# Expert weights loaded into dying attention buffers, a loop head at another slot, and two GpSimd steps at another time, in a two-layer decoder trunk

## What is computed

```python
def moe_swiglu(hn, w_router, w_gate, w_up, w_down):
    logits = (xt @ w_router).astype(jnp.float32)
    top_logit, top_idx = lax.top_k(logits, TOP_K)        # 2 of 8 experts
    gates = jax.nn.softmax(top_logit, axis=-1)
    ...
    def expert_block(args):
        xb, e = args
        hid = jax.nn.silu(xb @ w_gate[e]) * (xb @ w_up[e])
        return hid @ w_down[e]
    ...
    y = jnp.zeros((T, D), hn.dtype).at[row_tok].add(yb * row_g[:, None])
```

## Time and profile before

| | us |
|---|---|
| median of 3 runs | 1325.47 (1324.51 to 1325.51) |
| the profiled execution | 1328.43 |
| its span, first to last instruction | 1326.6 |
| PE busy | 1290.7 (97%) |
| DVE busy | 677.4 (51%) |
| ACT busy | 252.0 (19%) |
| POOL busy | 63.7 (5%) |
| mean granted TensorE clock | 0.996 |
| DMA over the span | 442.93 MB, 334 GB/s |

### The profile page before, as it was taken

The page is one execution under the profiler, slowest core; times in us unless marked ns, Lnnn a source line. Parts: engine busy times, 40 slices in busy tenths (PEclk is TensorE's granted clock), DMA queues, the critical chain, the costliest instruction groups (busy, mean ns, idle before and its releaser), DMA issues.

```text
span 1326.6 us, 38823 instructions
## 1 busy us (share of the span) xinstructions
PE 1290.7 (97%) x17222; PEld 1007.6 (76%) x17222; DVE 677.4 (51%) x943; ACT 252.0 (19%) x386; POOL 63.7 (5%) x50
## 2 busy tenths in 40 slices
PE   9999999999999999999999999999999999999898
PEld 9998899988767567567766955866875695696597
DVE  5875655554875556165145335516614614542661
ACT  5564544443643100000000000000000000000000
POOL 1001000000000330000000000000000000002600
PEclk9999999999999899999999999999999999999999
DMA  9867565565522999999999999999999999999992
GB/s 320 261 213 227 187 191 181 180 223 179 186 93 72 388 419 418 416 419 417 416 418 417 416 416 410 417 417 409 417 416 405 417 416 402 417 417 416 405 398 103
DMA packets 114224, 442.93 MB, mean 334 GB/s; under 512 B 9284, under 2 KB 55700, under 8 KB 83348
## 3 DMA queue, kind: packets, MB, share of 16 engines
q1 hardware_dynamic: 107904, 424.75, 81.3%
q10 hardware_dynamic: 4820, 11.53, 2.5%
q0 software_dynamic: 1344, 4.20, 0.8%
HBM read 434.12 MB, written 12.08 MB: 336 GB/s over the span
## 4 chain that ended last, share of the span: by engine, by line
PE 90%; DVE 4%; ACT 3%; issue 3%; DMA 0%; ACTq 0%; DVEq 0%
PE bank L2003 22%; PE bank L2051 22%; PE bank L2021 20%; PE bank L1553 7%; PE bank L1555 7%; PE bank L1554 7%; ACT w_hi L661 1%; DVE w_lo L955 1%; PE bank L1800 1%; PE bank L1711 1%; DMA const<-in_shape_constants 0%; PE bank L1976 0%; ACT ht_hi L689 0%; DVE sums L1478 0%; PE bank L1855 0%
## 5 line engine op out<-in xcount | busy, mean ns | idle before, releaser
L2003 PE MATMUL bank<-raw,xT 128*32 128x384 f32 (+1 forms) x2688 | 260.5, 532 | 10.7 <-issue 9.8
L2003 PEld LDWEIGHTS bank<-raw,xT 128*32 128x32 f32 x2688 | 110.8, 110 | 154.3 <-issue 133.8
L2021 PE MATMUL bank<-more_ring,xT 128*32 128x256 f32 (+1 forms) x3072 | 207.0, 354 | 0.4 <-issue 0.4
L955 DVE TENSOR_TENSOR w_lo<-raw,w_hi 128x2048 fp32r<-128x2048 f32 x62 | 141.4, 2289 | 98.0 <-ACT w_hi L661 98.0
L1473 DVE TENSOR_TENSOR sums<-more_ring 128x768 f32<-128x768 f32 (+1 forms) x64 | 69.8, 1090 | 234.3 <-PE bank L2021 193.3
L2051 PE MATMUL bank<-more_ring,hidT 128*32 128x256 f32 x3072 | 170.7, 379 | 0.0
L2021 PEld LDWEIGHTS bank<-more_ring,xT 128*32 128x32 f32 x3072 | 147.4, 110 | 25.2 <-issue 5.0
L2051 PEld LDWEIGHTS bank<-more_ring,hidT 128*32 128x32 f32 x3072 | 150.4, 110 | 18.1
L1553 PE MATMUL bank<-ht_hi,w_hi 128*128 128x256 f32 x464 | 128.7, 277 | 1.5 <-DVE ht_lo L969 1.5
L2051 PE MATMUL bank<-raw,hidT 128*32 128x256 f32 x2304 | 129.2, 379 | 0.0
L1555 PE MATMUL bank<-ht_hi,w_lo 128*128 128x256 f32 x464 | 128.3, 277 | 0.0
(11 more groups left out here) (312 smaller groups left out, 1603.1 us busy)
## 6 DMA issues: line engine op xcount, KB each, us to landing
more_ring<-in_moe_w_up SPq DMA_DIRECT2D x64, 1024.0 KB, 17.4
more_ring<-in_moe_w_down SPq DMA_DIRECT2D x64, 1024.0 KB, 16.2
raw<-in_moe_w_gate SPq DMA_DIRECT2D x64, 768.0 KB, 18.3
more_ring<-in_moe_w_up SPq DMA_DIRECT2D x64, 768.0 KB, 18.2
raw<-in_moe_w_gate SPq DMA_DIRECT2D x48, 1024.0 KB
raw<-in_moe_w_down SPq DMA_DIRECT2D x48, 1024.0 KB, 18.9
more_ring<-in_moe_w_gate SPq DMA_DIRECT2D x16, 1024.0 KB
raw<-in_hgrn_w_in SPq DMA_DIRECT2D x15, 1024.0 KB, 11.8
```

Source lines behind the costliest of these rows:

```text
L955: nc.vector.tensor_tensor(w_lo[:, slot, :], raw[:, slot_raw, :], plain(w_hi[:, slot, :]), SUB).then_inc(split_ready, 1)
L2003: ins = nc.tensor.matmul(out_banks[j][GTOK * c:GTOK * c + GTOK, 0:w], xT[:, j, kt, :], chunk[:, c], start=kt == 0, stop=kt == KT - 1)
L2021: ins = nc.tensor.matmul(dst[GTOK * c:GTOK * c + GTOK, :], rows, columns[:, c], start=opens, stop=pair == PAIRS - 1, skip_group_check=True)
```

## The change

Five edits, in SBUF layout and in waits; no computation is added or removed.

- `w_hi` and `w_lo` move up behind the first 16240 floats (`LOW`) of the region; the stage memory of the attention now starts at the bottom, right under `more_ring`, in the order `bias_rev`, `kT`, `aqT`, `vt`, and so on.
- SP issues the loads that follow the eight of `raw` when all logits are computed (12 signals of `logits_full`), and, from the first load on that reaches past `bias_rev`, `kT` and `aqT` (`KEYS_END`, load 12 in the code), when the attention products are done (`turned`). The waits for `chunk_used` and `h_part` go.
- The PE loop's head goes from slot 128 to slot 0.
- GpSimd waits, after its gathers, for all hidden-layer transposes of the last item before it multiplies and adds.
- Routing scratch (`hnT` and the small tensors) lies in the region of `w_lo`; `e_silu`, `e_hid` and `hidT` no longer share space with it as before, the small tensor `over` is renamed `over_cap`, and the scratch of a Square (L680) is a buffer of its own.

```diff
-LOOP_SLOT = 128
+LOOP_SLOT = 0
+
+LOW = 16240
...
-        dense = ExitStack()
-        w_hi = sb(dense, "w_hi", [P, SPLIT, CW], f32r)
-        w_lo = sb(dense, "w_lo", [P, SPLIT, CW], f32r)
+        with ExitStack() as over:
+
+            sb(over, "low", [P, LOW])
+            w_hi = sb(over, "w_hi", [P, SPLIT, CW], f32r)
+            w_lo = sb(over, "w_lo", [P, SPLIT, CW], f32r)
...
         bias_rev = sb(s, "bias_rev", [P, QH, 2 * P])
-        vt = sb(s, "vt", [P, TT, 256])
-
         kT = sb(s, "kT", [P, KVH, T])
         aqT = sb(s, "aqT", [P, QH // 2, T])
-
+        vt = sb(s, "vt", [P, TT, 256])
...
+        with ExitStack() as over:
+
+            sb(over, "below_lo", [P, LOW + SPLIT * CW])
+            hnT = sb(over, "hnT", [P, KT, T])
+            rank0 = sb(over, "rank0", [P, TT, E])
...
+        with ExitStack() as over:
+
+            squares = sb(over, "squares", [P, D])
+        early_second = sb(ctx, "early_second", [P, TT, D])
...
+        KEYS_END = QH * 2 * P + KVH * T + QH // 2 * T
...
-            sp.wait_ge(chunk_used, C_MOE)
-            sp.wait_ge(h_part, 3 * 4)
             for k in range(in_raw, N_UP):
+                if k == in_raw:
+                    sp.wait_ge(logits_full, 3 * KVH)
+                if k < first_lap and LOAD_ENDS[k - 1] <= RAW * CW + KEYS_END < LOAD_ENDS[k]:
+                    sp.wait_ge(turned, TURN_ATT)
                 if k >= first_lap:
                     wait_used(0, k)
                 load(0, k)
...
+            pool.wait_ge(hidT_ready, n_before * (2 * GRPS) + 2 * GRPS)
+            pool.sem_inc(pool_pace, 1)
             for i in range(2):
                 for t in range(TT):
                     pool.wait_ge(fetched[t][i], 16)
...
-                    spare = hidT[1][:, 0:2, :, :].rearrange("p g m t -> p (g m t)") if i == 3 else xs[:, t, :]
+                    spare = squares[:, :] if i == 3 else xs[:, t, :]
```

More of the change, by code:

```diff
@@ L254, in build_program @@
         s.close()
-        dense.close()
-        more_ring = sb(ctx, "more_ring", [P, RING - RAW * CW])
+        with ExitStack() as over:
+            sb(over, "below_lo", [P, LOW + SPLIT * CW])
+            hnT = sb(over, "hnT", [P, KT, T])
+            rank0 = sb(over, "rank0", [P, TT, E])
+            top = sb(over, "top", [P, TT, 8])
+            topi = sb(over, "topi", [P, TT, 8], u32)
+            topf = sb(over, "topf", [P, TT, 2])
+            hot = sb(over, "hot", [P, TT, 2, E])
+            mask = sb(over, "mask", [P, TT, E])
+            rank = sb(over, "rank", [P, TT, E])
+            big = sb(over, "big", [P, TT, E])
+            more = sb(over, "more", [P, 2, E])
+            which = sb(over, "which", [P, E + 1])
+            nth = sb(over, "nth", [1, 2, E])
+            whose = sb(over, "whose", [1, 2, E])
+            it = sb(over, "it", [1, 8, 2, E])
+            itf = sb(over, "itf", [1, 32])
+        more_ring = sb(ctx, "more_ring", [P, RING - RAW * CW])
+        ones = sb(ctx, "ones", [P, E + 1])
+        base = sb(ctx, "base", [P, E])
+        late = sb(ctx, "late", [P, E])
+        over_cap = sb(ctx, "over_cap", [P, E + 1])
+        steps = sb(ctx, "steps", [P, 44])
+        quarters = sb(ctx, "quarters", [P, 4])
+        with ExitStack() as over:
+            squares = sb(over, "squares", [P, D])
+        early_second = sb(ctx, "early_second", [P, TT, D])
         xT = sb(ctx, "xT", [P, GRPS, KT, GTOK])
@@ L260, in build_program @@
         slot = sb(ctx, "slot", [P, TT, 2, 4], u32)
-        steps = sb(ctx, "steps", [P, 44])
-        quarters = sb(ctx, "quarters", [P, 4])
         passed = sb(ctx, "passed", [P, TT, 2, 44])
@@ L269, in build_program @@
         end_selT = sb(ctx, "end_selT", [CAP, T])
[L270 to L294, removed]
+        e_silu = sb(ctx, "e_silu", [P, GRPS, 512])
+        e_hid = sb(ctx, "e_hid", [P, GRPS, 512])
+        hidT = [sb(ctx, f"hidT{i}", [P, GRPS, n // GTOK, GTOK]) for i, (at, n) in enumerate(SUPERS)]
         banks = [ctx.enter_context(nc.psum_tensor(f"bank{i}", [P, 512], f32)) for i in range(8)]
@@ L1339, in _ @@
             nc.vector.memset(ones[:, :], 1.0)
-            nc.vector.memset(over[:, :], 0.0)
+            nc.vector.memset(over_cap[:, :], 0.0)
             nc.vector.tensor_scalar(base[:, :], iota8, float(CAP), None, MUL)
@@ L1381, in _ @@
             then(ins)
-            then(nc.vector.tensor_tensor(over[:, 1:E + 1], more[:, 0, :], more[:, 1, :], ADD))
-            then(nc.vector.tensor_tensor_scan(which[:, :], ones[:, :], over[:, :], 0.0, MUL, ADD))
+            then(nc.vector.tensor_tensor(over_cap[:, 1:E + 1], more[:, 0, :], more[:, 1, :], ADD))
+            then(nc.vector.tensor_tensor_scan(which[:, :], ones[:, :], over_cap[:, :], 0.0, MUL, ADD))
             nc.vector.tensor_scalar(itf[0:1, 16:17], which[0:1, E:E + 1], float(E), None, ADD)
```

## The result

The changed kernel takes 1337.3 us (median of 5 runs, 1331.29 to 1339.31) beside 1325.47 us for the kernel before; the ratio over all runs is 1.0075, 95% interval 1.0059 to 1.0091. The profiled execution took 1331.29 us with a span of 1329.5, against 1328.43 and 1326.6 before: some 3 us more in the profiles, 10 in the ratio. The profile of after is thus the quickest of its runs, and I read it for places rather than for the total.

What follows compares the result with a forecast made beforehand. It took the expert loop as bound by TensorE, DMA queues nearly as full. Adds 3.0, slot 0.8 and loads 0.3 us off the median 1325.47 gave 1321.4, stated as 1321.0 (1319.3 to 1322.7 at 0.60; 8 in 10: 1317.3 to 1324.3).

Steps and rivals of the forecast that it cites:

- The new places of buffers: SBUF layout: moved buffers, routing scratch among them, keep every shape and instruction; costed at nothing.
- the list of what the new profile would show: Signs for each step: late adds, ordinary last item, DMA without pause from 415 us, small gap gone, items of 108.2 us.
- Slot 0: PE expert loop's head: the fetch boundary 62 records behind it goes away; 0 to 1.5 us gain, taken as 0.8.
- rival (3): Expert loop's two fast phases: an added boundary in each arrives late, 0.5 us each, 8 us in all, 1329.0; chance 0.08.
- three signs that I had named for a failure: Items over 109 us, a microseconds-long gap inside the last item's matmul run, or VectorE's last addition waiting for GpSimd.
- The adds: Last item's first fast phase: moving GpSimd's adds later frees VectorE's sums; 3.0 us in the median, up to 6.6 profiled.
- gap of 2.77 us in the profiled execution of before: Last item's first fast phase: PE issue gap taken as late code; with clock loss about 3.6 us, profiled execution only.
- my 22 us: VectorE beside GpSimd's eight instructions: full-length exclusion would cost some 22 us, sum near 1303; ruled out, given no chance.
- The early loads: SP's ten loads after the raw half: start 13 to 16 us earlier; gain between 0 and 2.7 us, taken as 0.3.
- Rival (4): First item's first fast phase: its 2.7 us vanish through the early loads, 1318.6; chance 0.18 together with another rival.
- The sum: Whole kernel against the median 1325.47: 3.0 + 0.8 + 0.3 = 4.1 us faster, 1321.4; stated as 1321.0.

Runs made afterwards that it cites:

- e4: Changed kernel with only its new buffer addresses: slot 128, early adds and SP's old waits as in the kernel before; 1341.01 us, ratio 1.0087.
- e1: Changed kernel with the loop head back at slot 128; 1332.35 us, ratio 1.0031 to the kernel before.
- e6: Changed kernel with weight splits 64 B higher (LOW = 16256) and loop head at slot 128; 1320.97 us, ratio 0.996 to the kernel before.
- e2: Changed kernel with its weight splits 64 B higher (LOW = 16256), nothing else; 1328.27 us, ratio 0.9997 to the kernel before.
- e5: Kernel before with the loop head at slot 0 and nothing else; 1332.65 us, ratio 1.0069.
- e3: Kernel before with GpSimd's multiplies and adds moved behind the last item's transposes, nothing else; 1325.07 us, ratio 0.9972.
- e7: e6 with SP's old waits ahead of the ten loads; 1320.93 us, ratio 0.9965 to the kernel before.

## Why the prediction was wrong

Against the kernel before, by single parts: new addresses +0.87% alone (e4), and +0.71% and +0.78% in the pairs e1 to e6 and after to e2; slot 0 +0.69% alone (e5), +0.44% and +0.37% in the pairs e1 to after and e6 to e2; late adds -0.28% (e3); early loads about 0 (e6 and e7). In a chain: e4 +0.87, adds and loads to e1 -0.56, slot to after +0.44, together +0.75%, which adds up by construction and checks nothing. The single parts, each alone on the kernel before, add up to +1.28%, more than the +0.75% measured: they aren't independent, and how they act on each other isn't shown. The entry gap of slot 0, from 2.0 to 5.9 us in three traces, is one thing that varies.

**The new places of buffers** were the step that failed. The prediction said that they "keep every shape and instruction. I cost them at nothing." They cost 0.7 to 0.9%, 9.4 to 11.5 us, more than everything else in the sum, by matmuls that came every 118.3 ns and not every 111.7. No rival covered it, and the list of what the new profile would show looked at nothing ahead of 415 us. The premise was true, same shapes and same instructions, and the conclusion wrong: an address is a part of an operand. I know of no row of before that gives the price, but a bound should have been set. The dense layers make up a third of the span, and every matmul in them reads a buffer that the change moves.

**Slot 0** had the wrong sign in the whole, though not in the items. The gain of 0.8 us was argued from the small gap 62 records behind the head, which does go, and the large gap at the head goes with it (1.4 us to none), more than I had. The first fast phase then holds gaps that come to 11.1 us over the eight items, 1.4 each, which is rival (3)'s mechanism at somewhat over its price of 1 an item, though in one of the two phases only. The items still came out shorter: from the second to the seventh they last 108.15 us on average in after, as the 108.2 that I had named, beside 108.54 before; 108.33 in e2 beside 108.49 in e6. Of the three signs that I had named for a failure one came, a gap of about a microsecond inside the run of matmuls in the last item (1.14 us at 1232.94); the items stayed under 109 us and VectorE's last addition waited for PE. The loss is where neither the sum nor rival (3) looked, at the loop's entry (2.0 us in after, 2.1 in e2, 5.9 in e5) and exit (1.9 to 2.0), with the clock loss behind a long gap. I had priced the boundaries inside the loop, and no path into and out of it. The Trainium skill (Runtime: NRT & Kernel Launch, Instruction fetch mechanics) has block crossings mostly hidden. The traces agree for the second plain phase and the down products, where no gap under "issue" shows at any slot, and not for the first fast phase, where a block lasts 5.39 us, nor for the first boundary close behind the head.

**The adds** were right in kind, place and size of the cover. They run from 1289.5 to 1310.6 beside L2062, the wait is harmless, nothing waits for them, and the gain is 3.7 us in e3's ratio, where I had 3.0. In the layout of after it may be more: e4 to e1 is 7.4 us, but in their traces 2.5 us of that stand ahead of the loop (entered at 456.34 and 453.80), where the adds can have no part. Two pieces of the reasoning behind it did not hold. First, e4 shows 6.1 us of excess and e5 6.7 from VectorE's sums, without a PE gap under "issue" of more than 0.3 us. So the gap of 2.77 us in the profiled execution of before was not a piece on top of a typical 3.0; it seems rather to have stood in place of one of these locks, which I can't show for the median runs. What that gap was stays open. Second, I wrote that the rule of the Trainium skill was "ruled out and gets no chance". In e4 a sum that starts beside a running GpSimd add ends 0.81 us after that add, twice, as it would if nearly all of its 0.95 us of work had to wait for the add's end. The kernel before shows the same. Its add from 1225.25 lasts until 1228.33, and this is the sum beside it:

```profile
1226.01 3.13 DVE L1478 TENSOR_TENSOR sums<-more_ring,sums 128x768 f32<-128x768 f32 x1
```

It ends at 1229.14, again 0.81 us after the add. The means that I read the earlier trace rows had hidden it: the 1956 ns of L1478 are one sum of 3.13 us, one of 1.79 and one of 0.95. So for these pairs the rule (the Trainium skill, SBUF — State Buffer, Who interferes with whom) holds. Only my 22 us was wrong: in e4 VectorE has twelve sums in that stretch and loses 5.9 us in four of them; the other eight take about 0.95 us each.

**The early loads** were right: the pause at 422 us is gone, and it is worth nothing that e7 could tell from zero. Rival (4), that they would shorten the first item, is out, since e7 has the short first item without them; what shortens it stays open.

**The sum** was 4.1 us faster. With the edits that I costed by what they turned out to be, -3.7 and +5.8, it would have been 2 us slower; with the addresses, 12 us slower, and 9.9 us was measured by the ratio. e6 shows what the change holds without its two losses: 1320.97 us, where 1321.0 was predicted for the change as it stood. That they meet so closely is luck: the sum held 0.8 us for a slot that e6 doesn't have, and the ratio gives e6 5.3 us where the other terms made 3.3.

## What to carry to other kernels

When a change moves buffers, note the addresses of each matmul's two operands modulo 128 B before and after, and count matmul records per window in both: 64 B were worth 0.7 to 0.8% here, and no idle time tells of it. After any edit that shifts code around a hardware loop, look at four places, the entry, the head, the first block boundary behind the head, and the exit, and at the block boundaries inside the phase that issues fastest. Look at single instructions before you price a contention by a mean: one sum in three may carry all of it. Price each edit from a row that could show it, and where none can, put a bound on it, not a zero.

## What the hardware showed

A 256-wide matmul came every 111.7 ns (179 records in 20 us) or every 118.3 ns (169), mainly by the relation of its two operands' addresses modulo 128 B (with all operands turned by 64 B the first layer had 172); a move by 128 B changed next to nothing (169 and 171). The loop head's slot alone moved the kernel between 0.996 and 1.0256 of the time before. By an inference from gaps, code at the target of a jump back was there about 4.5 us after the last block was entered, and the block behind it after about 10. A VectorE sum of 0.95 us was stretched to between 3.12 and 3.14 us beside a GpSimd add, and ended 0.81 or 0.82 us after it in five cases, and a GpSimd multiply of 2.85 us to 4.33 beside VectorE's sums.
